# The delta rule in chunks of 128 tokens instead of 64, with beta and the key norm as scales per token

## The reference, cut to what matters

```
a_mat = where(strict, (k * beta) @ k.T * decay, 0) + eye      # decay[i, j] = exp(G_i - G_j)
u, k_cum = solve(a_mat, [v * beta, k * beta * exp(G)])        # unit lower triangular
v_new = u - k_cum @ state
out   = (q * exp(G)) @ state + where(incl, q @ k.T * decay, 0) @ v_new
state = state * exp(G_last) + (k * exp(G_last - G)).T @ v_new
```

## Time and profile before

| | |
|---|---|
| time, median of 3 runs | 1131.43 us (1129.44 to 1131.69) |
| span of the profiled execution | 1127.7 us, 17514 instructions |
| TensorE busy | 1100.3 us, 98% |
| VectorE busy | 767.3 us, 68% |
| ScalarE busy | 556.2 us, 49% |
| mean DMA rate | 164 GB/s, main queue 45.9% of 16 engines |
| mean granted TensorE clock | 0.993 of full speed |

### The profile page before, as it was taken

One profiled execution on the slowest core, in us unless ns is written; L12 is line 12 of the kernel. 1 busy time (PEld: TensorE's weight loads), 2 busy tenths in 40 slices (PEclk: granted clock), 3 DMA queues, 4 the chain that ended last, 5 costly groups with the idle time before them and its releaser, 6 DMA issues.

```text
span 1127.7 us, 17514 instructions
## 1 busy us (share of the span) xinstructions
PE 1100.3 (98%) x7442; PEld 973.8 (86%) x7442; DVE 767.3 (68%) x937; ACT 556.2 (49%) x664; POOL 36.4 (3%) x98
## 2 busy tenths in 40 slices
PE   9989999999999999999998999999999999999997
PEld 8888998997989999998797888888888888888886
DVE  5486788554668998787677575556667866656555
ACT  6466564333535443445665454444455665444443
POOL 6000000000000000000003200000000000000000
PEclk9998999999999999999999999999999999999999
DMA  8542443333355555554453355555534435555551
GB/s 306 181 156 75 150 150 116 111 116 110 130 175 194 187 187 187 187 187 167 169 180 134 129 174 190 194 196 198 191 119 174 153 115 187 184 190 187 187 187 56
DMA packets 27455, 185.07 MB, mean 164 GB/s; under 512 B 3169, under 2 KB 3681, under 8 KB 5618
## 3 DMA queue, kind: packets, MB, share of 16 engines
q1 hardware_dynamic: 26208, 182.46, 45.9%
q10 hardware_dynamic: 1170, 1.49, 0.4%
HBM read 182.89 MB, written 1.05 MB: 163 GB/s over the span
## 4 chain that ended last, share of the span: by engine, by line
PE 89%; DVE 7%; ACT 2%; issue 1%; POOL 0%; DVEq 0%; ACTq 0%; POOLq 0%
PE ps L2041 12%; PE ps L2056 12%; PE ps L2043 12%; PE ps L1971 10%; PE ps L2009 9%; PE ps L2015 9%; PE ps L2010 9%; PE ps L1977 5%; DVE low L1299 2%; DVE arena L1466 1%; PE ps L2073 1%; PE ps L1991 1%; PE ps L2375 1%; PE ps L2237 1%; PE ps L2143 0%
## 5 line engine op out<-in xcount | busy, mean ns | idle before, releaser
L891 ACT ACTIVATE whi<-raw 128x2048 fp32r<-128x2048 f32 x170 | 324.3, 1913 | 333.1 <-PE ps L2056 165.8
L1299 DVE TENSOR_TENSOR low<-raw,whi 128x2048 fp32r<-128x2048 f32 x170 | 389.2, 2293 | 40.3 <-ACT whi L891 37.4
L2009 PE MATMUL ps<-hboth,whi 128*128 128x256 f32 x880 | 221.0, 289 | 3.3 <-ACT conv L980 3.3
L2010 PE MATMUL ps<-hboth,whi 128*128 128x256 f32 x880 | 217.0, 284 | 0.0
L2009 PEld LDWEIGHTS ps<-hboth,whi 128*128 128x128 f32 x880 | 169.4, 192 | 7.9 <-ACT whi L891 3.6
L2010 PEld LDWEIGHTS ps<-hboth,whi 128*128 128x128 f32 x880 | 169.7, 193 | 0.7 <-issue 0.2
L2041 PE MATMUL ps<-whi,ahi 128*128 128x512 f32 x416 | 164.2, 395 | 2.8 <-issue 1.9
L2043 PE MATMUL ps<-whi,alo 128*128 128x512 f32 x416 | 162.8, 391 | 0.0
L1971 PE MATMUL ps<-hboth,whi 128*128 128x512 f32 x512 | 128.1, 392 | 0.0
L2015 PE MATMUL ps<-hboth,low 128*128 128x256 f32 x880 | 124.2, 284 | 0.5 <-DVE low L1299 0.5
L2056 PE MATMUL ps<-low,ahi 128*128 128x512 f32 x416 | 119.7, 389 | 0.0
(11 more groups left out here) (376 smaller groups left out, 1216.1 us busy)
## 6 DMA issues: line engine op xcount, KB each, us to landing
raw<-in_ffn_up SPq DMA_DIRECT2D x32, 1024.0 KB, 4.8
raw<-in_ffn_down SPq DMA_DIRECT2D x32, 1024.0 KB, 4.9
raw<-in_w_up SPq DMA_DIRECT2D x22, 1024.0 KB, 4.9
raw<-in_w_gate SPq DMA_DIRECT2D x12, 1024.0 KB, 4.9
raw<-in_w_down SPq DMA_DIRECT2D x11, 1024.0 KB, 4.9
raw<-in_w_dn SPq DMA_DIRECT2D x6, 1024.0 KB, 4.9
raw<-in_w_sc SPq DMA_DIRECT2D x6, 1024.0 KB, 4.8
raw<-in_w_branch SPq DMA_DIRECT2D x6, 1024.0 KB, 4.8
```

The source lines that it names most:

```text
L891: act.activation(whi[:, u % SPLIT, :], raw[:, u % RAW, :], ACT.Copy).then_inc(sem("hi_done"), 1)
L1299: dve.tensor_tensor(wlo[:, u % RAW, :], raw[:, u % RAW, :], whi[:, u % SPLIT, :].bitcast(F32), ALU.subtract).then_inc(sem("lo_done"), 1)
L2009: pe.matmul(out, wh, hi[:, k0 + k, :], start=opens and k == 0, stop=False, skip_group_check=True)
L2010: pe.matmul(out, wh, lo[:, k0 + k, :], start=False, stop=False, skip_group_check=True)
```

## The change

The unit of work of the delta rule becomes one tile of 128 tokens. `dn_off` and `dn_join` add one level that joins the two 64 by 64 inverses of a tile to one of 128 by 128 (XF). There are two chunks and so one state, one update and one `dn_new`; the state needs no decay. The first tile needs no key product with a state, the second no state update. Beta and the inverse key norm no longer go through matrices made by TensorE and VectorE: they are factors per token, applied to rows (`bk`, `rk`) when PSUM is read. The decay factors are made for full 128 by 128 blocks, with the gate as broadcast weights and `tri` as moving data. The products of ones with a scaled triangle (lines 2203, 2204) go. `dn_tok` makes two scaled copies instead of three, `dn_pre` one product instead of three. ScalarE has a new copy in `dn_off`, and makes exp(G) and `dn_sol`'s copy for the second tile alone. `dn_out` of the first tile moves from index 66 to 67 and now stands ahead of `dn_sum` of the second tile. GpSimd makes two masks fewer and clears two corners more in the first 25 us. The lines taken out of the functions below stand in the functions printed above; dn_off of ScalarE copies 64 partitions by 256 elements, dn_join of VectorE negates as many.

```
-59: [("dn_z", 1, 5), ("dn_sol", 0)],
-60: [("dn_sol", 1), ("dn_new", 0)],
-62: [("dn_state", 0), ("dn_new", 1)],
-63: [("dn_state", 1)],
-65: [("dn_sum", 0), ("dn_new", 2), ("dn_state", 2)],
-66: [("dn_new", 3), ("dn_state", 3), ("dn_sum", 1), ("dn_out", 0)],
+59: [("dn_z", 1, 5), ("dn_off", 0)],
+60: [("dn_off", 1), ("dn_join", 0)],
+61: [("dn_join", 1), ("dn_sol", 0)],
+62: [("dn_sol", 1)],
+63: [("dn_state", 0)],
+64: [("dn_new",)],
+65: [("dn_state", 1), ("dn_sum", 0)],
+67: [("dn_out", 0), ("dn_sum", 1)],
...
     def dn_pre(t):
...
+        dve.tensor_tensor(reach[t], wide(tri[:, :].unsqueeze(1), [DH, P]),
+                          wide(rk[:, :, t].unsqueeze(2), [DH, P]), ALU.mult)
...
     def dn_decay(t):
...
+        dve.wait_ge(sem("dn_grow"), t + 1)
+        if t:
+            dve.wait_ge(sem("dn_eg"), 1)
+        for h in range(DH):
+            ins = dve.tensor_scalar(DT[t][:, h, :], ps[:, grow_bank[t], h * P:(h + 1) * P], gcol[:, t, h:h + 1],
+                                    0.0, ALU.subtract, ALU.min)
+        ins.then_inc(sem("dn_dt"), 1)
+        dve.wait_ge(sem("dn_edt"), t + 1)
+        link(dve.tensor_tensor(DT[t], DT[t], reach[t], ALU.mult))
+    def dn_kk(t):
+        dve.wait_ge(sem("dn_kked"), 2 * t + 1)
+        first, second = chunks
+        kk = ps[:, kk_banks[t][0], :]
         for c_ in chunks:
...
+            dve.tensor_tensor(LT[t][c_], packed(kk[c_], 0), DT[t][c_, :, c_], ALU.mult)
+        link(dve.tensor_tensor(Loff[t][first], packed(kk[first], 1), DT[t][first, :, second], ALU.mult))
         dve.wait_ge(sem("dn_kked"), 2 * t + 2)
...
+        link(dve.tensor_tensor(qkT[:, t], by(ps[:, kk_banks[t][1], :], DH), DT[t], ALU.mult))
+        dve.tensor_tensor(LT[t], LT[t], wide(bk[:, t, :].unsqueeze(2), [DH, CH]), ALU.mult)
+        ins = dve.tensor_tensor(Loff[t][first], Loff[t][first],
+                                bk[first, t, :].unsqueeze(2).to_broadcast([CH, DH, CH]), ALU.mult)
+        if t:
+            q = dnT[:, 0:DH, P:2 * P]
+            ins = dve.tensor_tensor(q, q, EG, ALU.mult)
+        own(ins, "dn_lt", t + 1)
...
     def dn_decay(t):
...
         if t:
...
+            pe.wait_ge(sem("dn_tok"), 4)
+        for h in range(DH):
+            ins = pe.matmul(ps[:, grow_bank[t], h * P:(h + 1) * P], gg[:, t, h:h + 1].to_broadcast([P, P]), tri[:, :],
+                            start=True, stop=True)
+        ins.then_inc(sem("dn_grow"), 1)
     def dn_kk(t):
         if t == 0:
...
+            pe.wait_ge(sem("dn_tok"), 2)
         else:
             pe.wait_ge(sem("dn_lt"), 1)
...
+        k_, q_ = dnT[:, DH:2 * DH, t * P:(t + 1) * P], dnT[:, 0:DH, t * P:(t + 1) * P]
+        first, second = chunks
+        for h in range(DH):
+            for c_ in chunks:
+                pe.matmul(ps[c_, kk_banks[t][0], h * CH:(h + 1) * CH], k_[:, h, c_], k_[:, h, c_],
+                          start=True, stop=True)
+        for h in range(DH):
+            ins = pe.matmul(ps[first, kk_banks[t][0], (DH + h) * CH:(DH + h + 1) * CH], k_[:, h, first],
+                            k_[:, h, second], start=True, stop=True)
+        ins.then_inc(sem("dn_kked"), 1)
+        for h in range(DH):
+            ins = pe.matmul(ps[:, kk_banks[t][1], h * P:(h + 1) * P], k_[:, h, :], q_[:, h, :],
+                            start=True, stop=True)
+        ins.then_inc(sem("dn_kked"), 1)
...
+        for h in range(DH):
+            for c_ in chunks[0:1] if l == LEVELS - 1 else chunks:
+                ins = pe.matmul(ps[c_, 2 * t + 1, h * CH:(h + 1) * CH], XT[t][c_, h, :], Y[t][c_, h, :],
+                                start=True, stop=True)
+        ins.then_inc(sem("dn_XBX"), 1)
         for h in range(DH):
             for c_ in chunks:
                 ins = pe.matmul(ps[c_, 2 * t, h * CH:(h + 1) * CH], Y[t][c_, h, :], XT[t][c_, h, :],
                                 start=True, stop=True)
         ins.then_inc(sem("dn_XBX"), 1)
+    def dn_off(t):
+        first, second = chunks
+        pe.wait_ge(sem("dn_X2"), 4 * (LEVELS - 2) + 2 * t + 1)
+        for h in range(DH):
+            ins = pe.matmul(ps[second, 7 - t, h * CH:(h + 1) * CH], Loff[t][first, h, :], X[t][first, h, :],
+                            start=True, stop=True)
+        ins.then_inc(sem("dn_off"), 1)
+    def dn_join(t):
+        first, second = chunks
+        pe.wait_ge(sem("dn_Yoff"), t + 1)
+        pe.wait_ge(sem("dn_X2"), 4 * (LEVELS - 2) + 2 * t + 2)
+        for h in range(DH):
+            ins = pe.matmul(ps[first, 2 * t + 1, h * CH:(h + 1) * CH], Y[t][second, h, :], XF[t][second, h, second],
+                            start=True, stop=True)
+        ins.then_inc(sem("dn_joined"), 1)
     def dn_sol(t):
...
+        pe.wait_ge(sem("dn_XF"), t + 1)
         for h in range(DH):
...
+            if t == 0:
+                ins = pe.matmul(ps[:, 1, h * P:(h + 1) * P], XF[0][:, h, :], vb[:, 0, h, :], start=True, stop=True)
+            else:
+                ins = pe.matmul(ps[:, 6, h * P:(h + 1) * P], rhsk[:, 1, h, :], XF[1][:, h, :], start=True, stop=True)
         ins.then_inc(sem("dn_solved"), 1)
+    def dn_state(t):
+        if t == 0:
+            pe.wait_ge(sem("dn_u"), 1)
+            for h in range(DH):
+                ins = pe.matmul(ps[:, 0, h * P:(h + 1) * P], kdec[:, 0, h, :], vb[:, 0, h, :], start=True, stop=True)
+            ins.then_inc(sem("dn_supd"), 1)
+            pe.wait_ge(sem("dn_X2"), 4 * (LEVELS - 1))
+        else:
+            pe.wait_ge(sem("dn_vnew"), 1)
         for h in range(DH):
...
+            ins = pe.matmul(ps[:, 2 + t, h * P:(h + 1) * P], qkT[:, t, h, :], vb[:, t, h, :], start=t == 0, stop=True,
+                            skip_group_check=True)
+        ins.then_inc(sem("dn_o"), 1)
+    def dn_new():
+        pe.wait_ge(sem("dn_u"), 1)
         for h in range(DH):
...
+            pe.matmul(ps[:, 1, h * P:(h + 1) * P], XF[1][:, h, :], vb[:, 1, h, :], start=h == 0, stop=False,
+                      skip_group_check=True)
+        pe.wait_ge(sem("dn_S"), 1)
+        pe.wait_ge(sem("dn_kcT"), 1)
+        for h in range(DH):
+            ins = pe.matmul(ps[:, 1, h * P:(h + 1) * P], kcT[:, h, 0:P], S[:, h, :], start=False, stop=True,
+                            skip_group_check=True)
         ins.then_inc(sem("dn_kS"), 1)
...
         for h in range(DH):
...
+            pe.matmul(ps[:, 3, h * P:(h + 1) * P], dnT[:, h, P:2 * P], S[:, h, :], start=h == 0, stop=False,
+                      skip_group_check=True)
```

More of the change, by code:

```diff
@@ L790, in _ @@
             made["ident"] = n[0]
-            for t_, v in ((ones, 1.0), (tri, 1.0), (blk64, 0.0), (cneg, 0.0), (dneg, 0.0)):
+            for t_, v in ((ones, 1.0), (tri, 1.0), (cneg, 0.0), (dneg, 0.0)):
                 then(pool.memset(t_[:, :], v))
@@ L820, in _ @@
             for c_ in chunks:
-                then(pool.tensor_copy(trip[c_, :], tri[c_, c_]))
                 then(pool.tensor_copy(idp[c_, :], ident[c_, c_]))
                 then(pool.tensor_copy(levp[c_, :, :], lev[c_, :, c_]))
+            for XF_ in XF:
+                then(pool.memset(XF_[chunks[1], :, chunks[0]], 0.0))
             made["delta"] = n[0]
@@ L1259, in _ @@
                          gate=gate, dn_cum=dn_cum, dn_decay=dn_decay, dn_x0=dn_x0, dn_y=dn_y,
-                         dn_sol=dn_sol, dn_out=dn_out, merge=merge, ple_gate=ple_gate, ple_p=ple_p,
+                         dn_off=dn_off, dn_sol=dn_sol, dn_out=dn_out, merge=merge, ple_gate=ple_gate, ple_p=ple_p,
                          ab_qk=ab_qk, ab_v=ab_v, lam=lam, pool_mm=pool_mm,
@@ L1638, in dn_new @@
-            def dn_new(c):
-                t, p0 = c // 2, CH * (c % 2)
-                if c == 0:
-                    return
-                dve.wait_ge(sem("dn_kS"), c)
-                part = vb[p0:p0 + CH, t]
-                own(dve.tensor_tensor(part, part, by(ps[p0:p0 + CH, 0, :], DH), ALU.subtract), "dn_vnew", c)
-            def dn_state(c):
-                if c == NCH - 1:
-                    return
-                t = c // 2
-                dve.wait_ge(sem("dn_supd"), c + 1)
-                pS = by(ps[:, 1, :], DH)
-                if c == 0:
-                    own(dve.tensor_copy(S, pS), "dn_S", 1)
-                    return
-                for h in range(DH):
-                    ins = dve.scalar_tensor_tensor(out=S[:, h, :], in0=S[:, h, :], scalar=gt[:, t, h, c % 2:c % 2 + 1],
-                                                   in1=pS[:, h, :], op0=ALU.mult, op1=ALU.add)
-                own(ins, "dn_S", c + 1)
+                rows_ = chunks[0] if last else slice(0, P)
@@ L2183, in dn_cum @@
                 for t in range(TT):
-                    for j, m in enumerate((tri64, blk64)):
+                    for j, m in enumerate((tri, ones)):
                         at = (2 * t + j) * DH
@@ L2198, in dn_decay @@
             def dn_decay(t):
-                pe.wait_ge(sem("dn_gb"), 2 * t + 2)
                 if t:
-                    pe.wait_ge(sem("dn_tok"), 6)
```

(9 more changed lines are left out.)

163 lines of the change are left out of this document (56 added, 107 removed).

## The result

The changed kernel took 1117.72 us (median of 4 executions, 1117.48 to 1119.39) against 1131.56 for the kernel before (4 executions, 1129.44 to 1133.86). The ratio is 0.9896, with an interval of 0.9878 to 0.9914. The profiled executions are 10.0 us apart, 1127.7 and 1117.7 in span. So there are two questions: why the trace has 10.0 and not 6.8, and where the other 3.8 are.

What follows compares the result with a forecast made beforehand. TensorE's queue, busy 98% of the span, was taken to bound the kernel. Terms -12.2 - 1.9 - 1.2 + 2.1 + 3.1 + 0.3 + 0.5 + 2.5 sum to -6.8 us: 1131.4 to 1124.6, range 1120.8 to 1128.6.

Steps and rivals of the forecast that it cites:

- state and update: TensorE's state stage: 18.7 us of slots become six groups of 8 instructions at 1.08 each, 6.5 us; -12.2 us.
- k k' and q k': TensorE's dn_kk: 1.09 us a tile becomes groups of 0.55, 0.52 and 1.08; two tiles, +2.1 us.
- last level and join: TensorE's last dn_z, dn_off and dn_join: six groups in a single 64 by 64 tile at 0.52 each; +3.1 us.
- interruptions: Steps between TensorE's half units: two more interruptions at 0.17 us each; +0.3 us.
- before dn_x0: TensorE's new wait for VectorE, x0 coming 2.2 us later and TensorE 0.95 later; +0.5 us, between 0 and 2.
- before unit 35: TensorE's new wait for the bank that ScalarE's sigmoid frees, behind dn_out(0) and dn_sum(1); +2.5 us, between 0 and 4.
- 2: Rival: the hole of 2.4 us before unit 35 lowers TensorE's clock, 2.4 us more, 1127.0 us; chance 0.12.
- 1: Rival: the wait before unit 35 is hidden by ScalarE's order or overlapping sums; -9.3 us, 1122.1 us; chance 0.13.
- 3: Rival: ScalarE's table switches each cost 1.4 us beyond the load, wait before unit 35 grows by 2.8, 1127.4 us; chance 0.03.
- 4: Rival: three dependent products of the two tiles' chain lose 1 us each to VectorE's split; -3.8, 1127.6 us; chance 0.10.
- 5: Rival: 96 full-array instructions wait for weight loads, 18 us more, 1142.4 us; gain gone above 0.206 an instruction; chance 0.04.
- 6: Rival: the change does little, as removed TensorE work was less than its slots show; chance 0.03.

Runs made afterwards that it cites:

- the two repeats: Kernel before and changed kernel, both unedited, run again on one chip: 1129.5 us (11 executions) and 1119.93 us (5 executions).
- experiment 8: Changed kernel with the state update reading 64 of 128 rows and the query's product with the state making 64 of 128 output rows: 1120.25 us, one execution.
- The repeats: The changed kernel unedited, run twice more beside the kernel before: 1119.93 us, ratio 0.9922, and on another occasion 1119.75 us, ratio 0.9904.
- experiment 4: Changed kernel with dn_cum half a unit earlier, at index 25 instead of 26: 1119.55 us.
- experiments 7 and 8: 7: changed kernel without dn_off and dn_join, 1118.47 us; 8: changed kernel with two groups on a part of the array, 1120.25 us.
- swapped kernels: Changed kernel with dn_sum(1) ahead of dn_out(0) at index 67, alone or with another move: alone 1116.24 us, repeated 1116.20 us.
- experiments 3, 6, 11 and 12: The changed kernel with dn_sum(1) ahead of dn_out(0): 1116.24 us; 6 also dn_cum half a unit earlier: 1116.42; 11 repeats 3: 1116.20; 12 has dn_x0 later: 1116.64.

## Why the prediction was wrong

| step | forecast | trace |
|---|---|---|
| state and update | -12.2 | 5.1 for 18.7: -13.6 |
| solve | -1.9 | 0.91 and 0.81: -2.3 |
| decay | -1.2 | 2.70 for 3.84: -1.1 |
| k k' and q k' | +2.1 | 1.99 for 1.09, twice: +1.8 |
| last level and join | +3.1 | +2.8 |
| interruptions | +0.3 | -0.1 |
| before dn_x0 | +0.5 | 0.32 and 0.24: +0.6 |
| before unit 35 | +2.5 | 2.14: +2.2 |
| sum | -6.8 | -9.7, of a span shorter by 10.0 |

The direction, the chance and the mechanism were right: TensorE's queue sets the time, and the new one is that much shorter. The sum can be checked without the slots: from the half unit at 122.70 us (123.48 after) to unit 35 (295.67 before, 286.67 after) the changed kernel gains 9.8 us on the kernel before. The same count between the two repeats gives 11.3, of which 1.7 is the fall at 259 us: 9.6. The executions have 9.2 to 9.5 by span times clock.

**The step that failed first** is the price of the full groups: "At 1.08 each", "priced by line 2298, which has 128 weight columns but 64 rows. Their upper end is 0.18 [...] nothing in the rows makes them cheaper than 0.13." Ten of the twelve took 0.81 to 0.91, near 0.11 an instruction; the second of the decay's, with a wait ahead of it and a change of shape behind, took 1.09. What was wrong with the row shows inside line 2298 itself, in the trace of the kernel before:

```profile
265.40 0.38 PE L2298 MATMUL ps<-arena 64*128 64x128 f32 x2
...
266.07 0.27 PE L2298 MATMUL ps<-arena 64*128 64x128 f32 x1
```

The first of the 8 instructions lasts from 265.19 to 265.40, 0.21 us, and the last one has 0.20 to the unit at 266.27; the six between them take 0.67, or 0.11 each. So the 1.08 holds two changes of shape, which a full group between full-size units doesn't have; experiment 8 brings them back by its edit alone, and the group's 0.2 with them. The full groups of the solve of tile 0 and of dn_kk have one change ahead of them and took 0.91. The kernel before also had full-size instructions back to back: the 8 transposes of line 2194 take from 177.17 to 178.14, a change of shape behind them included. "Nothing in the rows" is true of the rows that were picked, not of the trace. The price was wrong by 1.4 us in the state, 0.4 in the solve and 0.3 in dn_kk. The prediction had the parts in hand: it had found that changes cost 0.18 against 0.135, named the Trainium skill's rule for it (TensorEngine Tiling, Key Properties: changing the tiling mode drains the engine), and then left the changes in the price of groups that have none. The trace agrees with the rule, at 0.1 us on each side of a change.

The price of an interruption fails by the same step. The prediction took 0.17 from 3.06 less 2.89, but the half unit that it put at 2.89 takes 2.97 in the trace (269.25 to 272.22), since a change of shape follows it. A half unit alone takes 2.88 (274.68 to 277.56 in the changed kernel), so an interruption by small tiles costs 0.19, a change at either end; one by full-size groups costs 0.07 (2.95, 267.97 to 270.92). There are two interruptions more, but most of those in the state stage are now of the cheap kind: -0.1 in all for +0.3. The rest of the 2.9 us between the two sums is the single tile's price, 0.3 too high in the last level and join, and 0.3 in the wait before unit 35.

**The step that failed second** is the base: "what lies outside the span (3.8 us at the median) is the same". What lies outside is 1.7 to 1.8 us in every one of the executions since. The other 2.0 are as much as one level of the clock: the median of the first three executions was 2.0 above the profiled one. Against the 1129.3 of 26 later executions on one chip the same sum gives 1122.5 and the range 1118.7 to 1126.5, and the changed kernel's median is 1119.9 there. So what put the first result below the range was the base and the clock of two small samples; the first step, with the smaller terms, made the sum 2.9 us too small in either case. And the first sample of the changed kernel, 1117.7, was one with few falls. Its executions had clocks of 0.994, 0.996, 0.996 and 0.997. Its median is 1.7 under its profiled execution, and that of the kernel before 2.1 over its own: these are the 3.8 us by which 13.8 exceeds 10.0. The repeats have 9.3 and 10.4.

**The rivals.** 2, that the wait before unit 35 costs the clock, was given 0.12. A fall stood behind the wait in two of the changed kernel's three traces, 1.6 and 1.5 us in the stretch behind it where 2.4 were put down. It stood there in experiment 4 too, and not in experiments 7 and 8, which also have the wait: three of six. But the changed kernel's trace without one gave up as much elsewhere (5.1 against 5.0). The four traces of swapped kernels, without the wait, gave up two portions each and the six with it two or three, yet the mean clock is the same, 0.9946 over the 14 executions of the changed kernel and 0.9945 over the 20 of the swapped ones (experiments 3, 6, 11 and 12). So no extra time of the rival's is seen, and a few tenths of it can't be ruled out. 1 is out: the wait was there. 3 is out: ScalarE's sigmoid started 1.29 after its load. 4 is out, since no product of the state stage waited. 5 is out by its own number, 0.11 against the 0.206 from which it decides, and 6 with it. The estimates of both waits held, 0.56 for 0.5 and 2.14 for 2.4.

## What to carry to other kernels

Where one engine's queue has no holes, its slots can be added up to within some tenths, waits included; the price of a group needs to be read without its first and last instruction, from very short stretches of the timeline, and the changes of shape at its ends counted by themselves. Before a gain is added to a median, split the median: what is outside the span, and how low the mean clock was; span times clock told kernels apart here to some tenths, where a difference of two medians of 4 executions was off by 4.5. When a step is moved, walk the list of every engine that it passes: here two short steps in the other order on ScalarE were worth 3.5 us of 1120 by the medians and 2.4 to 2.7 in work.

## What the runs showed of the hardware

- fp32 instructions of 128 columns took 0.11 us one after the other on 64 rows and on 128. A change of shape cost about 0.1 us ahead of it and 0.1 behind: groups of 8 with one at both ends took 1.02 to 1.09 us, full-size ones with one ahead 0.91, and those with none 0.81 ahead of a unit and 0.88 to 0.90 ahead of another such group. A half unit took 2.88 us alone, 2.95 between full-size fp32 groups and 3.06 between groups on small tiles.
- A fall of TensorE's clock to the lower of its two levels gave up 1.7 us of full-speed time, or twice that at 105 us. It was found behind 32 products of one column (at 105 us, in all 14 traces but one), behind the wait of 2.14 us before unit 35 (in three of the six traces that have it), behind small tiles and a wait of 0.78 in the state stage of the kernel before (once in two), behind a wait of 2.2 us at 80 us (in six of the 14 traces, which all have that wait) and behind one of 1.4 us at 602 or 616 us (in three of the 14, which all have it). Falls that came in some executions of a kernel and not in others go with a spread of its times over 3 to 7 us.
- Five traces of the two kernels each gave up 5.0 or 5.1 us, at different places; those of the variants gave up between 1.7 and 5.1. Taking away one place where the clock fell, the wait before unit 35, did not raise the mean clock over the executions, 0.9945 without it and 0.9946 with it.
